# Moving gated-linear-attention chunks, half projection passes and a pooling chain inside a two-block transformer kernel

## The reference, cut to what matters

```python
p = einsum('btd,dc->btc', rmsnorm(x, norm_g), w_in)
(gq, gk, gv, gz, ggate, dq, dk, dv, dgate, qi, ki, wi, pu, pgate) = split_cols(p)
y_gla  = rmsnorm(gla_mixer(gq, gk, gv, glog), gla_norm_g) * silu(ggate)  # 4 heads, chunks of 64 tokens, a running state
y_dsa  = dsa_mixer(dq, dk, dv, qi, ki, wi, rel_bias) * silu(dgate)       # 6 heads, 256 best keys per query
y_pool = pool_mixer(pu, pool_w, pool_scale) * silu(pgate)                # sums over windows of 2, 4, 8, 16 tokens
x = x + concat([y_gla, y_dsa, y_pool]) @ w_out
```

## Time and profile before

| | |
|---|---|
| time, median of 3 | 2902.96 us (2902.62 to 2904.7) |
| the profiled execution | 2900.97 us, with a span of 2899.2 us |
| PE busy | 2788.4 us, 96% of the span |
| DVE busy | 1167.8 us, 40% |
| POOL busy | 1025.4 us, 35% |
| ACT busy | 903.2 us, 31% |

### The profile page before, as it was taken

One profiled execution on the slowest core, in us unless ns is written; L12 is line 12 of the kernel. 1 busy time (PEld: TensorE's weight loads), 2 busy tenths in 40 slices (PEclk: granted clock), 3 DMA queues, 4 the chain that ended last, 5 costly groups with the idle time before them and its releaser, 6 DMA issues.

```text
span 2899.2 us, 41295 instructions
## 1 busy us (share of the span) xinstructions
PE 2788.4 (96%) x16908; PEld 2168.4 (75%) x16908; DVE 1167.8 (40%) x2954; ACT 903.2 (31%) x1701; POOL 1025.4 (35%) x447
## 2 busy tenths in 40 slices
PE   7999898899999999998999999999999999999998
PEld 5766675677777777776887878888888888887787
DVE  7987897556433334335345011111112121114423
ACT  5322413552333433434123222222222222214112
POOL 2532491133322222223542433333333323333542
PEclk9999899999999999999999999999999999999999
DMA  4110021121211111112221111111111111114211
GB/s 116 37 30 23 22 72 56 66 74 38 67 38 38 51 52 52 52 44 88 66 72 56 54 44 37 44 45 44 37 48 48 37 45 44 44 37 146 66 51 66
DMA packets 221335, 155.57 MB, mean 54 GB/s; under 512 B 25254, under 2 KB 207948, under 8 KB 221020
## 3 DMA queue, kind: packets, MB, share of 16 engines
q1 hardware_dynamic: 210076, 122.55, 14.6%
q10 hardware_dynamic: 11072, 30.39, 3.0%
HBM read 133.45 MB, written 19.47 MB: 53 GB/s over the span
## 4 chain that ended last, share of the span: by engine, by line
PE 50%; DVE 1%; issue 1%; ACT 1%; DMA 0%; ACTq 0%; DVEq 0%
PE proj L907 14%; PE proj L909 14%; PE proj L908 14%; PE out L1426 2%; PE score L1374 1%; PE score L1404 1%; PE score L1383 1%; PE proj L947 1%; PE out L908 0%; PE out L907 0%; PE out L909 0%; PE out L1393 0%; DMA y_scratch<-arena 0%; DVE arena L2406 0%; DVE arena L2533 0%
## 5 line engine op out<-in xcount | busy, mean ns | idle before, releaser
L907 PE MATMUL proj<-act_hi,w_hi 128*128 128x512 f32 x2560 | 1032.2, 403 | 10.5 <-ACT hT L1849 4.4
L909 PE MATMUL proj<-act_hi,w_lo 128*128 128x512 f32 x2560 | 1004.4, 392 | 0.0
L908 PE MATMUL proj<-act_lo,w_hi 128*128 128x512 f32 x2560 | 1003.8, 392 | 0.0
L780 POOL TENSOR_TENSOR w_hi<-w_raw,ones 128x1024 fp32r<-128x1024 f32 x175 | 420.8, 2404 | 1587.6 <-PE proj L909 1585.9
L907 PEld LDWEIGHTS proj<-act_hi,w_hi 128*128 128x128 f32 x2560 | 485.3, 190 | 123.6 <-issue 17.8
L909 PEld LDWEIGHTS proj<-act_hi,w_lo 128*128 128x128 f32 x2560 | 484.6, 189 | 104.7
L908 PEld LDWEIGHTS proj<-act_lo,w_hi 128*128 128x128 f32 x2560 | 485.9, 190 | 95.6 <-issue 0.2
L782 POOL TENSOR_TENSOR w_lo<-w_raw,w_hi 128x1024 fp32r<-128x1024 f32 x175 | 433.3, 2476 | 13.7
L1849 ACT ACTIVATE arena<-proj 128x512 f32<-128x512 f32 x236 | 175.9, 754 | 662.7 <-PE proj L909 638.7
L2533 DVE SCALAR_TENSOR_TENSOR arena<-arena,score 128x256 f32<-128x256 f32 (+1 forms) x192 | 76.1, 427 | 718.1 <-PE score L1374 677.3
L1875 ACT ACTIVATE arena<-score 128x512 f32<-128x512 f32 (+3 forms) x264 | 115.7, 487 | 194.2 <-PE score L1235 194.1
(11 more groups left out here) (292 smaller groups left out, 2994.0 us busy)
## 6 DMA issues: line engine op xcount, KB each, us to landing
w_raw<-dil_w_in_dram SPq DMA_DIRECT2D x80, 512.0 KB, 3.7
w_raw<-fox_w_in_dram SPq DMA_DIRECT2D x32, 512.0 KB, 4.1
w_raw<-w_in_dram SPq DMA_DIRECT2D x23, 512.0 KB, 3.8
y_scratch<-arena ACTq DMA_DIRECT2D x21, 512.0 KB, 3.7
act_lo<-y_scratch SPq DMA_DIRECT2D x21, 512.0 KB, 6.2
arena<-decay_scratch ACTq DMA_DIRECT2D x16, 512.0 KB, 5.7
w_raw<-ple_w_gate_dram SPq DMA_DIRECT2D x16, 512.0 KB, 3.7
arena<-x_dram SPq DMA_DIRECT2D x12, 512.0 KB, 4.7
```

Source lines behind the costliest of these rows:

```text
L780: pool.tensor_tensor(hi, raw, one.unsqueeze(1).broadcast_to([P, KB, P]), ALU.mult).then_inc(w_hi_done, 1)
L907: pe.matmul(bank, hi, a_hi, start=first, stop=False)
L908: pe.matmul(bank, hi, a_lo, start=False, stop=False)
L909: return pe.matmul(bank, lo, a_hi, start=False, stop=last)
```

## The change

1. `GLA_ROUNDS`: row 4 keeps its ten chunks; row 5 takes 14 instead of 16, with two or three rounds between them instead of two, and its last chunk at a new place, 33; row 6 takes 8 instead of 6, two to three rounds apart. Places 32 and 33 are new calls of `beside` in the closing operations of `threshold`.
2. `TURNED_AT`: the six gated outputs move from rounds 24, 25, 27, 29, 30 of row 6 and round 1 of row 7 to place 33 of row 6 and rounds 0, 7, 11, 12 and 15 of row 7.
3. `inverse_roots` moves from round 13 to 24 of row 6, `pool_outputs(0)` from 13 to 25 and `pool_outputs(1)` from 26 to 32 of row 7.
4. PE makes six half passes of pair 1 ahead of the attention; pair 1's two turns and two gate half passes go to the beginning of pair 0's attention, and all eight half passes of pair 2 into the loops of pair 0's and pair 1's attention, half a half pass in every step.
5. ACT makes the high parts of tiles 20 and 21. POOL's window chain is placed ahead of tiles 21 and 22 rather than 21 to 24. The scaling at line 843 gets a second operation, a multiplication by 1.0.
6. ACT stores the two pooled outputs at two places instead of one.

```diff
-GLA_ROUNDS = {4: range(12, 32, 2), 5: range(0, 32, 2), 6: range(0, 12, 2)}
-TURNED_AT = {(6, 24): 0, (6, 25): 1, (6, 27): 2, (6, 29): 3, (6, 30): 4, (7, 1): 5}
+GLA_ROUNDS = {4: range(12, 32, 2), 5: (0, 3, 5, 8, 10, 13, 15, 18, 20, 23, 25, 28, 30, 33), 6: (1, 4, 7, 9, 12, 15, 18, 21)}
+TURNED_AT = {(6, 33): 0, (7, 0): 1, (7, 7): 2, (7, 11): 3, (7, 12): 4, (7, 15): 5}
...
-    n = (4 if p == 0 else 8) + t // 4
-    turned = [unit(6 + t // 3)] if p == 1 and t in (0, 3) else []
-    return turned, (unit(n, t // 2 % 2) if t % 2 else None), None, []
+    if p == 0:
+        return [], unit(t // 2, t % 2), None, []
+    turned = [unit(4 + t // 2)] if t in (4, 6) else []
+    return turned, unit(4 + t // 2 if t < 4 else 6 + t // 2, t % 2), None, []
...
-        HI_BY_ACT = (0, 1, W_FOXF + 1, W_FOXF + 2, W_DIL + 1, W_DIL + 2)
+        HI_BY_ACT = (0, 1, W_DSA + 4, W_DSA + 5, W_FOXF + 1, W_FOXF + 2, W_DIL + 1, W_DIL + 2)
...
-                    pool.tensor_scalar(dst[rows, :], src[rows, :], pfix[rows, b, 16:17], None, ALU.mult).then_inc(windows, 1)
+                    pool.tensor_scalar(dst[rows, :], src[rows, :], pfix[rows, b, 16:17], 1.0, ALU.mult, ALU.mult).then_inc(windows, 1)
...
-                       19: (lambda: gates((0, 1, 2)),), 20: (lambda: gates((3, 4)),), 21: (first_windows,),
-                       22: (lambda: pooled(0, win_a, win_b, 4, 22),), 23: (second_windows,),
-                       24: (third_windows, lambda: pooled(1, win_c, win_b, 16, 24))}
+                       19: (lambda: gates((0, 1, 2)),), 20: (lambda: gates((3, 4)),),
+                       21: (first_windows, lambda: pooled(0, win_a, win_b, 4, 21)),
+                       22: (second_windows, third_windows, lambda: pooled(1, win_c, win_b, 16, 22))}
...
-                        project(2, [(b, half, None) for b, half in PAIR_HALVES[2:3]])
+                        project(1, [(b, half, None) for b, half in PAIR_HALVES[6:8]])
...
-                        project(2, [(b, half, None) for b, half in PAIR_HALVES[3:4]])
+                        project(1, [(b, half, None) for b, half in PAIR_HALVES[8:]])
...
-                    project(1, halves[0:4])
+                    project(1, halves[0:2])
                     pool_products(0)
-                    project(1, halves[4:])
-                    project(2, halves[0:2])
+                    project(1, halves[2:5])
                     pool_products(1)
+                    project(1, halves[5:6])
                     bias_tables()
...
+                    weight_hi(W_DSA + 4, C_DSA + 3)
...
+                    weight_hi(W_DSA + 5, C_DSA + 5)
...
-                          (4, 8): chunk_keys, (6, 13): inverse_roots, (7, 13): lambda: pool_outputs(0), (7, 26): lambda: pool_outputs(1)}
+                          (4, 8): chunk_keys, (6, 24): inverse_roots, (7, 25): lambda: pool_outputs(0), (7, 32): lambda: pool_outputs(1)}
...
                 count(0.0, over, ALU.is_gt)
+                beside(i, 32)
...
                 small(dve.tensor_tensor_scan(flag, ones[:, 0:1].broadcast_to([P, w]), flag, over, ALU.mult, ALU.add))
+                beside(i, 33)
```

More of the change, by code:

```diff
@@ L1886, in pair @@
                     if kind == "dsa" and p == 0:
-                        projected(2, 2, [(b, half, None) for b, half in PAIR_HALVES[2:4]])
+                        projected(1, 1, [(b, half, None) for b, half in PAIR_HALVES[6:]])
                     if p > 0:
@@ L1973, in attention @@
                     projected(0, 0, halves[4:6])
+                    weight_hi(W_DSA + 4, C_DSA + 3)
                     gates((4,))
                     projected(0, 0, halves[6:])
-                    projected(1, 1, halves[0:4])
+                    weight_hi(W_DSA + 5, C_DSA + 5)
+                    projected(1, 1, halves[0:2])
                     store_gla()
+                    projected(1, 1, halves[2:4])
+                    load_bias()
+                    store_pool(0)
                     projected(1, 1, halves[4:5])
-                    load_bias()
-                    projected(1, 1, halves[5:])
+                    store_pool(1)
+                    projected(1, 1, halves[5:6])
                     act.wait_ge(GL["mmul"], 5)
-                    projected(2, 2, halves[0:2])
-                    for b in range(2):
-                        store_pool(b)
                     bias_tables()
```

## The result

The changed kernel takes 2918.05 us (median of 5 runs, 2914.39 to 2919.98), the kernel before 2904.66 us beside it (2902.62 to 2905.49). The ratio is 1.0046, with a 95% interval of 1.0031 to 1.006: slower by 9 to 17 us. The profiled execution took 2919.98 us with a span of 2918.2 us, so it is the slowest of the five. The forecast of 2913 us lay 5 us under the median, inside its range.

The account below looks back on a forecast made before the run. PE, busy 96% of the span, bounds the kernel, so only its idle time and clock count, with DVE late; -10.7 + 19.8 + 1.4 = +10.5 us on 2900.97 gives 2911.5, stated as 2913 against the median, range 2897 to 2922.

Parts of the forecast that it names:

- Step 1: Key search rows 5 and 6: DVE's waits for chunks nearly go, so row 6 ends at 366.0, 26 us earlier.
- Step 2: Fifth `turn_output`: PE waits 13.6 us for a gated output, putting the sixth transposes at 393.4, 16 us later.
- Step 3: POOL's pooling chain: scaling 2.4 us, PE waits 6.7 us for tile 22, row 0 transposes at 463.9, 10.7 earlier.
- Step 4: Attention of pairs 0 and 1: four half passes moved into it cost 19.8 us, bounds 12.4 and 23.5.
- Step 5: PE's lower clock after waits: four waits over 3 us against three before, costing 1.4 us.
- Balanced: Pooling scalings run at 1 us and attention gaps are filled by 3 us more: +1.5, 2904 us; chance 0.25.
- Faster: PE does not stand at the fifth transpose; the search's end decides, row 0 26.6 us earlier: -6.8, 2896 us; chance 0.15.
- POOL decides: The second operation makes a pooling scaling 6.1 us, 14.8 us more on the chain: 2928 us; chance 0.08.

Follow-up runs that it names:

- e1: Changed kernel with its six gated outputs placed where DVE can make them at once, row 6's end to round 3 of row 7: 2919.45 us.
- e5: Changed kernel with gated outputs as in e1 and pooled outputs after rounds 12 and 22 of row 7 instead of 25 and 32: 2912.57 us.
- e7: Changed kernel with one half pass in step 3 of the attention of pairs 0 and 1 moved behind the scores and second transposes: 2913.38 us.
- e8: Changed kernel with the edits of e6 and e7 together: 2898.63 us, ratio 0.9983 to the kernel before.
- e4: Changed kernel with the pooling chain's scalings given one operation instead of two: 2928.59 us.
- b1: Kernel before with the change's chunk schedule, `inverse_roots` and `beside` calls, e1's gated outputs, and pooled outputs after round 17 and at place 33 of row 7: 2889.76 us.
- e6: e5 with all four half passes of pair 1 ahead of the second scores on PE, and their copies ahead of exp(0) on ACT: 2903.36 us.
- b2: b1 with the two-operation scaling in the pooling chain added: 2884.12 us, ratio 0.9932 to the kernel before.

## Why the prediction was right, point by point

**Step 1, chunks: right.** Row 5 ended at 284.1 against 285.8, row 6 at 366.8 against 366.0; PE left the GLA products at 327.4 against 329.5, within its bounds. DVE's waits for the chunks of rows 5 and 6 came to 2.8 us, where I had left 1.0. Row 6 itself took 82.7 us, where I had 80.2: I had taken POOL to be quiet there, but the last operation of the row, beside a pass of POOL, took 2.44 us instead of 0.39.

**Step 2, gated outputs: right in size, wrong in weight.** The wait of 13.3 us stood at the fifth `turn_output` (13.6 predicted), and the sixth transposes at 393.2 (393.4). But I called all that is behind it late by 16 us. e1 and e5 removed it and moved row 0 by 1.4 and 3.1 us. It was not on the path, as two later points (the rounds of the pooled outputs, and row 7's end through exp(0)) held PE anyway.

**Step 3, the pooling chain: the value was wrong, the sum right by luck.** The scaling took 1.12 us, not 2.4. It lay under my lower bound of 1.9 and under the 1.5 that I had named as a sign of being wrong. The sentence on the Trainium skill ("GPSIMD Engine Reference", Engine selection: one-input work at roughly line rate) had led to an estimate of 0.9 us; the trace comes near it for the scaling with two operations (1.12 us) and is far from it for the one with a single operation (2.8 to 3.1 us). PE's wait for tile 22 was 1.1 us, not 6.7. Those 5.6 us came back as the 5.84 us behind exp(0), and the half pass behind that wait took 8.0 us instead of 5.5, so that row 0 stood at 464.8 against my 463.9. I had checked DVE's end against PE (5 us of cover, and row 7 did end at 447.0, in my 445 to 450), but only for the transposes. The check that failed is who else waits for that end: exp(0) on ACT, with a copy queued behind it that PE needs for a gate half pass ahead of the transposes.

**Step 4, the attention: the mechanism incomplete, +27.2 against +19.8.** Of the 7.4 us, 1.7 are busy time (23.6 against 21.9; pair 1 had a granted clock of 0.95, and 0.97 before), and the rest is idle time that I had falling by 2.1 and that grew by 3.6. e7 shows where it arose: the half passes moved POOL's split onto DVE's minimum. In e8, where that is mended, the growth is 20.8, with 1.4 us of idle time filled: near my 19.8 and within its bounds. The 27.2 measured lie above my upper bound of 23.5.

**Step 5, clock: not tested by itself.** Half passes at the lower clock are in the trace behind each of the long waits (the one at 449.29 took 8.0 us, not 5.5), which is 2.5 us for one wait where I had 1.4 for a balance of all.

**The rivals.** "Balanced" had the scaling right and the time wrong, because what POOL gave was taken by the wait behind exp(0). "Faster" would have needed no wait at the fifth transposes, and also the new order around exp(0), which it did not name; with both, its sum nearly holds: it had row 0 26.6 us earlier and 19.8 us lost behind it, and e8 has 25.2 (474.6 less 449.4) and 20.8, and was measured 5 us under the kernel before. But its working does not: row 7 lasted 79.3 us in e8 and not 74.6, and ended at 447.8 and not at 440.6, and row 0 followed 1.6 us later and not 7.4 (8.1 in the trace of the kernel before). "POOL decides" gave the time of e4, 2929, by coincidence: its scalings of 6.1 us did not occur, and of the 10.5 us that e4 lost only 5.2 at row 0 are traced to its scalings of 2.9 us, which also hold up DVE.

**What the change is worth in parts.** The chunks, with outputs placed to suit them, brought DVE's end forward by 19 us and are worth 12 to 19 us without the rest (b1). In b1, PE transposes row 0 11.2 us after row 7's end, in e6 and e8 1.6 us after: 9.6 us is all that moving PE's work behind this point can bring. Moving four half passes does that (449.4 in e8 against 458.5 in b2), and costs 116.7 - 99.0 = 17.7 us in the pairs, so the move loses 8.6 us at the start of pair 2 even at its best (10.0 against b1, whose pairs took 97.5 us). By the ratios, 0.9983 against 0.9932 and 0.9945, it loses 15 and 11 us; what these are over 8.6 and 10.0 is within the 8.2 us by which the profiled executions differ behind the start of pair 2. The place of the window chain, `inverse_roots` and the two stores on ACT were not tried by themselves.

## What to carry to other kernels

A wait that is found in a trace, however long, costs only what the next gate behind it leaves: before it is given a price, follow every engine's queue from the late operation (here row 7, exp(0), a copy behind it, PE) and see which gate closes last. Work moved behind a point pays for itself only up to the slack of that point, and costs nearly its whole length (20.8 of 21.9 us here) if the place it goes to is already 90% busy. A moved half pass also moves the transfers and splits that its end releases; look at what they will run beside.

## What the runs showed of the hardware

**A second operation makes GpSimd's scaling faster.** The tensor-by-scalar product of 64x1024 floats took 1.12 us with `mult, mult 1.0` in all runs that had it, and 2.8 to 3.1 us with one `mult`, in the kernel before and in e4: 2.6 times as long for less arithmetic. Why is not settled.

**Operations of VectorE wait for a pass of GpSimd.** DVE's minimum over 128x256 took 0.48 us alone and ended 0.2 us behind POOL's pass when it met one; the closing operations of row 7 took 3.19 and 3.25 us beside POOL's split in the changed kernel and 1.23 each in the kernel before, and the split's two passes 3.79 and 3.20 us instead of 2.4. The minimum reads two operands in SBUF, and the Trainium skill ("SBUF — State Buffer", SBUF: two separate sides) says that the shared port pair is an exclusive lock, taken also by a DVE operation with two SBUF inputs when the GpSimd operation reads SBUF: the trace agrees, to 0.2 us.

**The clock differs in an untouched stretch.** In a stretch that begins 129.5 us behind the start of pair 2 and ends 2 us ahead of the next attention's first transposes (790.83 us before, 772.18 in b2), PE's granted clock was 0.90 in the kernel before, and 0.98 in b2 with the same code. Windows of before, then of b2:

```profile
700.00:789.00 89.00, 78.12 (x328) 60.60 (x327) 45.46 (x75) 31.38 (x52) 23.94 (x12) 0.90 0.18 48
```

```profile
687.00:770.00 83.00, 72.13 (x327) 55.78 (x326) 45.54 (x76) 31.18 (x51) 23.53 (x12) 0.98 0.19 52
```

That is 6 us for the same work, as much as what separates b1 from b2; the change does not touch this stretch. What sets the clock there is open.
